# A fused two-block transformer step on one core: the first block's weight rests move to VectorE, and the convolution's projections ahead of v

## What is computed

```
h = rms_norm(x, norm1_w) * (1 + scale1) + shift1        # scale, shift: silu(c) @ w_ada
q, k, v, cb, cc, cx, iq, ik, iw = split(h @ w_in)        # x: 256 tokens x 1024
score = sum_heads(relu(iq . ik) * iw)                    # index scores, causal
sel   = top_k(score, 64)
y_attn = softmax(rms(q) . rms(k) over sel) @ v
y_conv = cb * causal_conv3(cc * cx)
y_mix  = concat(rms_norm(y_attn), rms_norm(y_conv))
x = x + gate1 * (y_mix @ w_out)
...                                                      # expert layer, two more layers
```

## Time and profile before

| | |
|---|---|
| median of 3 runs | 1179.83 us (1178.1 to 1179.93) |
| the profiled execution | 1179.42 us, span 1177.5 us |
| TensorE busy | 1049.6 us (89%) |
| VectorE busy | 847.9 us (72%) |
| ScalarE busy | 433.2 us (37%) |
| GpSimd busy | 304.5 us (26%) |
| the part that the change touches | from 40 to 146 us of the span |

### The profile page before, as it was taken

How to read it: one execution, slowest core, us unless ns; L and a number is a source line. 1 busy time by engine, 2 the same in 40 slices (tenths; PEclk the granted TensorE clock), 3 DMA queues, 4 the chain that set the end, 5 groups by cost and what they waited for, 6 DMA issues and landing times.

```text
span 1177.5 us, 18884 instructions
## 1 busy us (share of the span) xinstructions
PE 1049.6 (89%) x7587; PEld 979.1 (83%) x7587; DVE 847.9 (72%) x1787; ACT 433.2 (37%) x913; POOL 304.5 (26%) x303
## 2 busy tenths in 40 slices
PE   8999987999999977878777888878999999999997
PEld 6999986998899877878777778868899888898885
DVE  6998989677667667667776766655755868765776
ACT  3644842123212221222222122212557654476452
POOL 1471005343334333333333343434000000300000
PEclk9999999999999999999998998999999999999999
DMA  9965888999999999999999999999954655455540
GB/s 370 406 228 197 329 298 313 420 421 421 420 420 421 421 421 421 419 422 420 422 421 420 422 420 421 421 420 420 366 203 166 230 210 181 149 209 179 188 169 36
DMA packets 59481, 390.36 MB, mean 332 GB/s; under 512 B 6785, under 2 KB 7809, under 8 KB 15618
## 3 DMA queue, kind: packets, MB, share of 16 engines
q0 software_dynamic: 36864, 268.45, 55.0%
q1 hardware_dynamic: 21056, 120.10, 27.6%
q10 hardware_dynamic: 1474, 0.60, 0.2%
HBM read 388.08 MB, written 1.05 MB: 330 GB/s over the span
## 4 chain that ended last, share of the span: by engine, by line
PE 55%; DMA 29%; DVE 9%; ACT 4%; issue 2%; SPq 0%; DVEq 0%
DMA rows<-in_peer_uv,work 25%; PE aux L1568 20%; PE pj L1611 5%; PE pj L1613 5%; PE pj L1612 5%; PE pj L1288 4%; PE pj L1290 4%; PE pj L1289 4%; PE aux L1547 3%; DMA rows<-in_w_ada 2%; DVE rows L2053 2%; DMA low_pairs<-in_peer_uv,work 1%; DVE rows L1759 1%; ACT work L1144 1%; DVE low_pairs L1770 1%
## 5 line engine op out<-in xcount | busy, mean ns | idle before, releaser
L1568 PE MATMUL aux<-work,rows 128*128 128x128 f32 x2080 | 261.7, 290 | 76.3 <-ACT work L1144 76.3
L1568 PEld LDWEIGHTS aux<-work,rows 128*128 128x128 f32 x2080 | 254.7, 205 | 84.0 <-ACT work L1144 83.8
L1568 PE MATMUL aux<-work,low_pairs 128*128 128x128 f32 x2016 | 238.1, 279 | 28.4 <-ACT work L1144 28.2
L1568 PEld LDWEIGHTS aux<-work,low_pairs 128*128 128x128 f32 x2016 | 232.9, 195 | 32.1 <-ACT work L1144 32.0
L900 POOL DMA_INDIRECT rows<-in_peer_uv,work x130 | 125.6, 966 | 299.6 <-PE aux L1568 231.2
L706 DVE TENSOR_TENSOR wlo<-wring,whi 128x1024 fp32r<-128x1024 f32 x100 | 121.0, 1234 | 77.6 <-ACT whi L700 77.1
L900 POOL DMA_INDIRECT low_pairs<-in_peer_uv,work x126 | 118.5, 940 | 156.0 <-PE aux L1568 151.3
L1139 ACT ACTIVATE work<-work 128x4 f32<-128x4 f32 (+2 forms) x71 | 14.7, 207 | 360.2 <-DVE work L2053 360.2
L1288 PE MATMUL pj<-xh,whi 128*128 128x256 f32 x512 | 147.0, 287 | 0.2
L1290 PE MATMUL pj<-xh,wlo 128*128 128x256 f32 x512 | 145.5, 284 | 0.0
L1289 PE MATMUL pj<-xl,whi 128*128 128x256 f32 x512 | 145.5, 284 | 0.0
(11 more groups left out here) (289 smaller groups left out, 1502.9 us busy)
## 6 DMA issues: line engine op xcount, KB each, us to landing
wring<-in_w SPq DMA_DIRECT2D x76, 1024.0 KB, 4.9
rows<-in_w_ada SPq DMA_DIRECT2D x40, 512.0 KB, 10.1
low_pairs<-in_w_ada SPq DMA_DIRECT2D x1, 4096.0 KB, 13.3
rows<-in_w SPq DMA_DIRECT2D x3, 1024.0 KB, 10.5
rows<-in_peer_uv,work POOLq DMA_INDIRECT x130, 17.4
work<-in_late_rows SPq DMA_DIRECT2D x2, 1024.0 KB, 7.6
xT<-in_gate_rows SPq DMA_DIRECT2D x2, 1024.0 KB, 7.3
rows<-in_norm_rows SPq DMA_DIRECT2D x2, 1024.0 KB, 7.5
```

The lines of the kernel that those rows point to most:

```text
L1568: ins = mm(peer_sum[t][:, c * P:(c + 1) * P], pair(n)[:, D + c * P:D + (c + 1) * P], diag[:, n % PICKS, :], start=(n % (EXPERT_HEADS * PIC ...
```

## The change

Four things are changed, all in the first block. All rests are made by VectorE, and the 14 of GpSimd are spread over VectorE's queue between the index scores, the picks and the ada tiles. The projections come in the order q, k, cc, cx, cb, v. v's two halves are TensorE's last projection work, with the sums of the convolution's squares (`sum_conv`) between them; these sums have a PSUM place of their own in `aux`. ScalarE's `round_to` calls and the order of its other steps follow that order, with the first of them now `round_to(5)` ahead of the relus.

```diff
-for name in ("q", "k", "v", "cc", "cx", "cb"):
+for name in ("q", "k", "cc", "cx", "cb", "v"):
     UNITS_1 += halves(name)
...
-LO_1 = "d" * 2 + "p" * 14 + "d" * 16
+LO_1 = "d" * 32
+LOWS_AMONG_PICKS = (6, 7, 7, 8, 8, 9, 10, 11)
...
-        conv_sums = chunk_out(M1 - KC + 2)
+        conv_sums = aux[:, 4, 0:T]
...
-            for n in range(2, 16):
-                split_lo(pool, "p", n)
...
-            round_to(3)
+            round_to(5)
...
-            round_to(4)
             for c in range(4):
                 take(qn[:, c, :], sq_to=sq[:, c, :])
-                if c % 2:
+                if c:
                     round_to(c + 5)
...
-            for t in range(NT):
-                take(v1[:, t, :], width=512)
-                round_to(14 + 2 * t)
-            qk_root(1)
             for c in range(4):
                 take(cc[:, c, :])
                 if c == 1:
-                    act.wait_ge(inv_k_turned, 1)
-                    nc.scalar.copy(inv_k_T[0:NT * HEADS, :], aux[0:NT * HEADS, 2, 0:P]).then_inc(inv_k_out, 1)
-                if c % 2:
-                    round_to(c + 17)
+                    round_to(14)
+                    qk_root(1)
+            round_to(16)
+            act.wait_ge(inv_k_turned, 1)
+            nc.scalar.copy(inv_k_T[0:NT * HEADS, :], aux[0:NT * HEADS, 2, 0:P]).then_inc(inv_k_out, 1)
...
+            act.wait_ge(conv_sum, 1)
+            nc.scalar.activation(rstd[:, :], conv_sums, ACT.Sqrt, bias=eps[:, 0:1], scale=1.0 / 512).then_inc(conv_std, 1)
+            for t in range(NT):
+                take(v1[:, t, :], width=512)
+                round_to(25 + t)
...
             qk_sums(0)
-            token_major(h_in)
+            whole(h_in, 2)
             qk_sums(1)
...
+            def sum_conv():
+
+                pe.wait_ge(att1["p_out"], 6)
+                for c in range(HC):
+                    pe.wait_ge(conv_sq, c + 1)
+                    ins = mm(conv_sums, ones[:, :], sq[:, c, :], start=(c == 0), stop=(c == HC - 1))
+                ins.then_inc(conv_sum, 1)
+
+            token_major(h_in, sum_conv)
...
+            pe.wait_ge(taken_act, M1 - KC)
             sum_v(att1, pt_buf, v_of_head, tiles=(0, ))
...
-            ada_dots(2 * KC, 2 * KC + ADA_RING)
+            for n in range(2):
+                ada_dots(2 * KC + n, 2 * KC + n + 1)
+                low_to(3 + n)
+            ada_dots(2 * KC + 2, 2 * KC + ADA_RING)
...
+                if n == 2:
+                    low_to(5)
+                if n == HEADS - 1:
+                    low_to(6)
...
+                low_to(LOWS_AMONG_PICKS[n])
...
-            y_over_sums(0)
             ada_dots(3 * KC + ADA_RING + 1, 3 * KC + ADA_RING + 2)
             dve.wait_ge(conv_std, 1)
...
+            low_to(26)
+            y_over_sums(0)
             y_normed(0)
-            conv_low(0)
             y_over_sums(1)
-            conv_low(1)
-            conv_low(2)
-            conv_low(3)
+            for c in range(HC):
+                conv_low(c)
             y_normed(1)
```

More of the change, by code:

```diff
@@ L499, in build @@
         w_hi = sem("w_hi")
[L500 removed]
+        w_lo = {"d": sem("w_lo_dve")}
         h_split, mix_hi, mix_split = sem("h_split"), sem("mix_hi"), sem("mix_split")
@@ L540, in build @@
         stored = sem("stored")
-        BANKS_1 = [2] * 3 + [2, 1, 1] + [2] * 2 + [1] * NT + [2] * 6 + [2] * 4
-        OWN_1 = ["a"] * (4 + 2 + 4 + 4 + NT + 4 + 4 + 4) + ["d"] * 8
+        BANKS_1 = [2] * 3 + [2, 1, 1] + [2] * 2 + [2] * 6 + [1] * NT + [2] * 4
+        OWN_1 = ["a"] * (4 + 2 + 4 + 4 + 4 + 4 + 4 + NT) + ["d"] * 8
         M1 = len(OWN_1)
@@ L1025, in _ @@
                 take(u[:, c, 2:T + 2])
-            round_to(22)
+            round_to(18)
             exps(att1, p_buf, 0, scale=inv_q)
@@ L1029, in _ @@
                 take(u[:, c, 2:T + 2])
-            round_to(25)
+            round_to(20)
             exps(att1, p_buf, 1, scale=inv_q, heads=range(0, HEADS // 2))
-            round_to(26)
+            for c in range(2):
+                take(cb[:, c, :])
+            round_to(22)
             exps(att1, p_buf, 1, scale=inv_q, heads=range(HEADS // 2, HEADS))
-            for c in range(HC):
+            for c in range(2, HC):
                 take(cb[:, c, :])
+            round_to(24)
+            nc.scalar.activation(warm[:, :], eps[:, 0:1], ACT.Sqrt)
             p_out(att1, pt_buf, 0)
+            p_out(att1, pt_buf, 1)
             for c in range(HC):
@@ L1039, in _ @@
                 nc.scalar.activation(sq[:, c, :], cc[:, c, :], ACT.Square).then_inc(conv_sq, 1)
-            nc.scalar.activation(warm[:, :], eps[:, 0:1], ACT.Sqrt)
-            p_out(att1, pt_buf, 1)
+            act.wait_ge(conv_sum, 1)
[3 more added lines that the diff above has]
+                round_to(25 + t)
             def y_root(t):
@@ L1059, in y_hi_part @@
                 nc.scalar.copy(xh[:, 0:HC, ts], yaT[:, :, ts]).then_inc(mix_hi, 1)
-            act.wait_ge(conv_sum, 1)
-            nc.scalar.activation(rstd[:, :], conv_sums, ACT.Sqrt, bias=eps[:, 0:1], scale=1.0 / 512).then_inc(conv_std, 1)
-            y_root(0)
-            round_to(27)
             for c in range(HC):
@@ L1067, in _ @@
                 nc.scalar.copy(xh[:, HC + c, :], cc[:, c, :]).then_inc(mix_hi, 1)
+            y_root(0)
             round_to(28)
@@ L1315, in whole, with token_major @@
                     ins.then_inc(proj, done)
-            def token_major(x):
+            def token_major(x, between):
                 m = chunk[0]
@@ L1321, in token_major @@
                 for half_ in range(2):
+                    if half_ == 1:
+                        between()
                     w = part_pairs(next_pieces(2))
@@ L1474, in _ @@
             logits(att1, q1, k1)
-            whole(h_in, 4)
+            whole(h_in, 2)
             whole(h_in, 4)
             turn_p(att1, p_buf)
+            def sum_conv():
[5 more added lines that the diff above has]
+            token_major(h_in, sum_conv)
             def v_of_head(h, k):
                 return v1[:, k, head1(h) * DH:(head1(h) + 1) * DH]
+            pe.wait_ge(taken_act, M1 - KC)
             sum_v(att1, pt_buf, v_of_head, tiles=(0, ))
-            bank_free(pe, M1 - KC + 2)
-            for c in range(HC):
-                pe.wait_ge(conv_sq, c + 1)
-                ins = mm(conv_sums, ones[:, :], sq[:, c, :], start=(c == 0), stop=(c == HC - 1))
-            ins.then_inc(conv_sum, 1)
             sum_v(att1, pt_buf, v_of_head, tiles=(1, ))
@@ L1862, in by_head @@
                 return z.rearrange("p (t c s) -> p t s c", c=HC, s=2)
+            low_to(12)
             dve.wait_ge(qk_std, 2)
@@ L1869, in _ @@
             chain.mark(v.tensor_tensor(qk_weight[:, :], cols[:, Q_W:Q_W + 1], cols[:, K_W:K_W + 1], ALU.mult))
-            ada_dots(2 * KC + ADA_RING, 2 * KC + 2 * ADA_RING)
+            ada_dots(2 * KC + ADA_RING, 2 * KC + ADA_RING + 1)
+            low_to(14)
+            ada_dots(2 * KC + ADA_RING + 1, 2 * KC + ADA_RING + 3)
             dve.wait_ge(inv_k_spread, 1)
@@ L1884, in mask_logits @@
                 chain.wait()
-            lowered[0] = 16
-            low_to(20)
-            ada_dots(2 * KC + 2 * ADA_RING, 3 * KC + ADA_RING)
-            ada_bias(2 * KC, 3 * KC)
+            low_to(16)
+            ada_dots(2 * KC + ADA_RING + 3, 2 * KC + 2 * ADA_RING)
+            low_to(18)
             dve.wait_ge(keep_ready, 2)
@@ L1893, in _ @@
                 v.scalar_tensor_tensor(smax[:, t, :], smax[:, t, :], -1.0, inv_q[:, t, :], ALU.mult, ALU.mult).then_inc(att1["negmax"], 1)
-                low_to(22 + 2 * t)
+                if t == 0:
+                    ada_dots(2 * KC + 2 * ADA_RING, 2 * KC + 2 * ADA_RING + 2)
+            low_to(20)
+            ada_dots(2 * KC + 2 * ADA_RING + 2, 3 * KC + ADA_RING)
+            ada_bias(2 * KC, 3 * KC)
             def over_sums(s, y, t, l=None):
@@ L1913, in _ @@
                                                       cc[:, c, :], ALU.mult, ALU.add))
-            base = 4 + 2 + 4 + 4 + NT
+            low_to(22)
+            base = 4 + 2 + 4 + 4
             for c in range(HC):
```

5 lines of the change are left out of this document (2 added, 3 removed).

## The result

| kernel | median us (runs) | before, same chip | ratio, 95% interval |
|---|---|---|---|
| changed | 1186.19 (5) | 1179.83 | 1.0055 [1.0042, 1.0069] |

The change costs 6.4 us, 0.55%; 0.8 was predicted, with 1183.4 as the upper end. The profiled execution took 1186.84, with a span of 1184.9.

A forecast was written before the change was run, and what follows sets the result against it. TensorE was taken to bound the touched part. Losses of 6.7 less 5.95 given back made +0.75, walking both queues 1.2, taken as +1.0: median 1180.6 from 1179.83, range for 8 in 10 1178.4 to 1183.4.

The forecast's parts named there:

- hi 4 and the relus: ScalarE's hi 4 waits for unit 5, so relus begin at 50.2 and q's fourth piece at 54.35: loss 2.5.
- The rival of the clock at the new gap: Clock drops behind TensorE's new idle time at 51.8, costing 3.4 less 1.25; time 1182.8; chance 0.1.
- Rests 6 and 7: TensorE waits for VectorE's rests near 63 and 67 us, 0.65 and 0.6: loss 1.25, between 0.9 and 2.0.
- cb's third piece: Rest 18 done at about 107.0, TensorE ready at 107.1: nothing lost; 1.3 if ScalarE's table load came behind the wait.
- Gap at 87: TensorE's late transpose of k's inverse norms (2.6) and the clock drop behind it (1.65) disappear: gain 4.25.
- Start of v: VectorE's rests 20 and 21 end at 116.1, TensorE ready at 115.9: loss 0.5, between 0 and 1.5.
- v behind everything: Sums over v must wait until v's last tile is taken: loss 0.85, where 0.4 was lost before.
- The tail: Ada tiles 29 and 30 ahead of the reciprocal delay TensorE's transposes by 0.9 and products by 0.7: loss 1.6.
- A change ahead can only move them as a whole: The 1011.8 us behind 165.71 us, where no instruction is changed, can only shift together.
- VectorE becomes the bound: Between 50 and 140 us each rest or round takes 0.1 more on VectorE: 1182.6 to 1183.4; chance 0.17.
- It does not act: Rests were hidden on GpSimd anyway and VectorE pays back what it saves: 1179.5 to 1180; chance 0.15.

The follow-up runs named there:

- the ada tiles: Changed kernel with the two ada tiles ahead of the reciprocal of the convolution's norm put behind its normalising; 1182.77, ratio 1.0028.
- the order alone: Changed kernel with rests 2 to 15 back on GpSimd, leaving only the new order of the projections; 1185.89, ratio 1.0061.
- the idle products at two places: Changed kernel with idle products at TensorE's three waits between 130 and 139 us and its wait near 178; 1186.51, ratio 1.0046.
- the delayed kernel: Kernel before with seven idle products (3.0 us) on TensorE at 150 us, between two pairs of output products; 1182.62, ratio 1.0039.
- the second profiles: Both kernels run again unaltered: changed kernel 1187.64, ratio 1.0064; kernel before 1180.62, ratio 1.0005 to itself.
- relus first: Changed kernel with unit 4's hi copy on ScalarE put behind the six relus instead of ahead; 1183.24, ratio 1.0032.
- the rests alone: Kernel before with its projections in the old order and only GpSimd's 14 rests moved to VectorE; 1188.72, ratio 1.0084.
- three small moves: Changed kernel with unit 4's hi copy behind the relus, two ada tiles behind the normalising, convolution's low halves earlier; 1178.29, ratio 0.9992.
- the repaired ones: Changed kernel with three repairs, 1178.29; also with three idle products near 178 us, 1178.78; also with v's first sums awaiting only its first tile, 1178.34.

## Why the prediction was wrong

Most waits were right. What failed is what the clock does behind them, the size of the tail, and what the kernel before was taken to lose. The working of each step is in the prediction. Two slips of its arithmetic change nothing: 120.0 and 5.6 are 125.6 and not 126.0, and its chances add up to 1.02.

**hi 4 and the relus (2.5): right.** 2.5 to 2.6 in three profiles. In time it is worth 2.7 (1.0055 less 1.0032), give or take 2 by the two intervals.

**The rival of the clock at the new gap (0.1): the step that failed first.** The wait at 52 was argued away because TensorE is busy on both sides of it. Of seven profiles with this wait and nothing in it, five show the fall (two of the three unaltered ones, the ada tiles, the order alone, the idle products at two places). The piece then takes up to 4.6 instead of 3.1 us from its first start to its last end. The rests hide part: there is no wait at 66 any more. Filling the wait gave 0.8 us, within the uncertainty, so what this fall costs in the median is not shown.

**Rests 6 and 7 (1.25): too high,** 0.6 in the first profile, all of it at rest 7. The 0.3 to 1.1 for `affine_select` did not come. Against it cb's third piece, counted at nothing, starts 0.6 late: the two ada tiles at 93.2 took 3.3 for 2.3, which I put down to GpSimd's multiplication beside them.

**Gap at 87 (gain 4.25): the step that was most wrong.** The gap is gone, as forecast, and the full clock stays. But 2.6 + 1.65 was the loss of one execution. Three others (the last is the delayed kernel's) wait 1.4, with no fall: that gives back about 1.5. The 5.04 in the earlier trace rows was two instructions, the second caught behind one more rest. Idle products in this gap changed nothing that could be told, so the median has little of the 1.65 for the clock in it; and their profile has the short form too, so the long wait stands in one of five.

**Start of v (0.5), v behind everything (0.85): right in kind,** 0.8 and 0.85.

**The tail (1.6): mis-sized.** Tile 29's landing came at 126.4 for 126.0, as forecast. But tile 30 was counted as being there. In the seven other profiles in which these tiles stand where the change has them, it lands 2.3 to 2.6 behind tile 29, and the transposes wait 1.9 to 2.1 instead of 0.7 (where idle products fill the wait, they start as late). Then the clock falls in the output products in seven of the eight profiles in which nothing was repaired at the tail, and costs 0.9 to 1.5 more (5.1 to 5.7 us from the transposes of the first tile to those of the second, 4.2 where it did not fall). Taking the tiles away gave 3.2 us (1.0055 less 1.0028), give or take 2.

**As a sum,** for the second profiles: relus 2.6, the fall behind them 1.5, cb 0.6, v 0.8 + 0.85, the tail 3.0, the fall in it 1.3: 10.65. Given back 1.5 + 1.7 = 3.2. That makes 7.45, and 151.31 - 144.10 is 7.2. Against the forecast's 0.75 the gap has 2.75 of the difference, the two falls 2.8, the tail 1.4, and the other terms cancel.

**"A change ahead can only move them as a whole": wrong for the first pair, and not quite right on the mean.** The 4.5 us of the first pair behind 146 us are mostly chance: the two other profiles of the changed kernel have spacings of 1031.7 and 1032.7, where those of the kernel before have 1031.0 to 1031.2. The first profile has one of its falls at 179, which made the fourth gather wait 1.48 us:

```profile
193.46 1.96 POOL L898 DMA_INDIRECT rows<-in_peer_uv,work  x1 [1.48 <-PE aux L1554]
```

This lateness need not remain. The kernel before has a fall at 174 in its third profile, and its twelfth gather is issued 19.27 us behind the first, here 19.28; yet it ends 995.2 behind the first gather, here 999.2. Another fall, at 814, comes close ahead of the last of the 256 gathers. The three profiles with a fall from 812 to 818 (changed, relus first, idle products at both places) issue the last gather 636.3 to 637.9 us behind the first, the fifteen others at most 634.9. But every profile has many falls between 200 and 810, and nothing was run against this one, so that it cost the time is argued and not shown.

That a late start grows by half or more in the gathers (theory C) is refuted by the delayed kernel, 995.8 and 995.0 us, and by the second profiles: the changed kernel's first gather is 7.6 us later than that of the kernel before, and its end 7.7. Over all profiles, though, the six with the old order have spacings of 1031.0 to 1031.7 (the delay taken off), and the twelve with the new order 1031.0 to 1035.5, 1.4 us more on average. So about that much of the 6.4 to 7.9 us lies behind the first addition, up to 0.4 of it at the reciprocal of the last section. Whether the new order meets costly falls there more often is open.

**VectorE becomes the bound (0.17)** is not what happened to the changed kernel, but it is to the rests alone. **It does not act (0.15)** is true of one half: rests on VectorE or GpSimd make no difference in the new order that the intervals could show. Not tried: the old order with the rests placed where each piece needs them.

## What to carry over

A loss that is read from one profiled execution is not yet a loss: where its end hangs on which of two instructions meets a neighbour's, take a second profile before booking it as a gain, and put idle work in the wait to see whether the fall behind it is in the median. A wait that is put on TensorE where it had been busy can cost more than its length, because the clock may fall behind it, as in five of the seven profiles above; price a new wait of 2 us with a fall, and count each transfer that stands ahead of a critical instruction by its own landing. Then repair the waits one by one: here three small moves gave back all that the reordering had lost.

## What had not been expected of the hardware

A VectorE addition of two SBUF operands lasts 1.25 us beside GpSimd's rests and 0.34 without them. Beside them three products with a tile of `w_ada` take 1.96 each on average, where they take 1.22 otherwise (order alone, VectorE's groups). The Trainium skill, SBUF — State Buffer (Who interferes with whom), says that such instructions and GpSimd's exclude each other; this agrees, while the picks, with one operand, kept their 1.17 a round.

The reciprocal of the second norm starts 0.37 us later behind the same ScalarE instruction in the changed kernel and the repaired ones, in each of their profiles (VectorE idle for 1.53 us ahead of it instead of 1.16), and not in the kernel before nor with either half alone. I have no cause for it.
